# Four dense units a layer in the GLA fronts instead of the RWKV beats, and modulation products in four column groups

## The chip, the cores and the metric

The kernel runs on one core of a Trainium2 chip. Its time is device time in microseconds (us) from the start of the program to its end, the median of three runs. TensorE multiplies matrices, ScalarE (ACT) and VectorE (DVE) work on elements, GpSimd (POOL) does little here, and SyncE (SP) issues the DMA transfers of the weights. Every tensor is float32.

## The reference, cut to what matters

Two layers of a trunk with three parallel branches (RWKV-7, gated linear attention, latent attention) run over 128 context tokens and 512 latent tokens. The kernel handles both as 640 columns.

```python
def adaln_project(x, cvec, norm_g, w_mod, b_mod, w_in):
    mod = (jax.nn.silu(cvec) @ w_mod + b_mod)[:, None, :]      # the modulation: 1024 -> 3072
    shift, scale, gate = jnp.split(mod, 3, axis=-1)
    h = rmsnorm(x, norm_g) * (1 + scale) + shift
    return h @ w_in, gate                                      # the dense projections
# layer_forward: proj is split into r, k, v, g ... of RWKV, q, k, v, g of GLA, qd, kvd, g of MLA, merge
    o_a, st_rw = rwkv7_branch(...)     # a scan over tokens, done in chunks of 128
    o_b, st_gla = gla_branch(...)      # chunks with decay, two directions
    ...                                # MLA: attention over latents and a cache
    y = (g_a * y_a + g_b * y_b + g_c * y_c) @ lp['w_out']
    return x + gate * y, (ckv, ml_kpe, st_rw, st_gla)
```

## The kernel before, in words

Activations stand transposed, as 128 channels by 640 tokens. Weights come as **units** of 128 x 1024 numbers (512 KB) through `ring`, a buffer of five units: SyncE issues unit n when TensorE has released unit n - 5. The order of all units is fixed in `STREAM`, made by `unit_order`. A **dense unit** gives one tile of 128 output channels: eight products of 128 x 128 weights with 512 tokens, and eight with the other 128 tokens. In the profile each float32 product is two MATMUL records, and each transpose (L555) is one.

The stages of a layer, in order:

1. The modulation of layer 0 (`mod_product`, `mod_turn`, `mod_columns`), only at the start of the program. Six groups of 512 outputs; in each, eight products of a 128 x 2 weight block (`sc`, the two conditioning vectors) with 512 columns of a modulation unit add up in `psum[0:2]`. ScalarE copies the two rows to `con_sb`, TensorE turns them into columns by four transposes, and VectorE copies those to `mod_new`. The transfers of `hT` (the tokens) and `small_sb` are issued by GpSimd when groups 0 and 4 are filled.
2. RWKV. 20 steps (`STEPS`, four pairs of heads by five chunks) and one more for the tail; each step has 13 **beats** (`SLOTS`). In a beat TensorE does `rounds(q, j)`, the j-th link of a dependent chain of small products that go through ScalarE or VectorE after each link, and `chain(q - 1, j)`, then `beat()`: what `beat_work` has put there. That is a tile (one 512-token product of a dense unit of `DENSE`); behind a unit's eighth tile come its eight 128-token products, the **rest part**. In layer 0, products of layer 1's modulation stand there too.
3. The units `kvd` and `gg` 0, then the **GLA fronts**, one for each (p, d): TensorE computes `gx` (16 rows), projects the unit `GLA_KEYS[p, d]`, waits for `dve_ki`, transposes the keys (`kit`), waits for ScalarE's copy of them, computes the state products `gs` (128x64 tiles), and then for each of seven or eight levels j the small products `att` j, which need `dve_kq` j, followed by a tile of the unit `GLA_LEVEL[p, d]`. VectorE makes `ki`, `level(0)`, `level(1)`, the gate of the projected unit, the four states from `gs`, and then in a loop over j `kq` j and `level(j + 2)`. ScalarE's `Exp` of a level stands between `level(j)` and `kq` j.
4. MLA, the branch outputs with their merge gates, and `w_out`.

PSUM banks go round in `ticket`, which waits until the bank's last content has been taken out. A matmul whose output has at most 32 rows is placed on the column group of the array that its first PSUM row names, so `psum[0:2]` is always the first of four.

## Time and profile before

| what | value |
|---|---|
| median of 3 runs | 2998.87 us (2989.98 to 3000.86) |
| time of the profiled execution | 3000.72 us |
| its span, first to last instruction | 2998.9 us |
| TensorE busy | 2708.9 us, 90% |
| VectorE busy, ScalarE busy | 1153.9 us, 1000.0 us |
| RWKV beats, layer 0 and layer 1 | 110.8 to 806.6 us, 1603.0 to 2231.5 us |
| GLA fronts, layer 0 and layer 1 | 825.7 to 1004 us, 2251.9 to 2428 us |

The profiled execution took 1.85 us more than the median, and 1.8 us of its time lie outside its span. The stages are told apart by the forms of TensorE's instructions: small products of 32 x 32 are the beats, and 16-row products begin a front. A matmul's end in the profile is modelled and lies some 0.17 us behind the start of what follows it in a stream, so from start to start is the better measure of a short stretch.

### The profile page before, as it was taken

Reading aid. Unit: us, or ns where it says so; the run is one execution under the profiler, and the core shown is the slowest. Engines: PE = TensorE matmul, PEld = TensorE weight load, DVE = VectorE, ACT = ScalarE, POOL = GpSimd, SP = SyncE. Lnnn points to the kernel's source line nnn. Section 1 sums busy time; section 2 is a strip of 40 time slices with the busy share of each in tenths; the row PEclk is TensorE's granted clock in tenths of the full one; section 3 lists DMA queues with packets and bytes.
Section 4 is the critical chain, followed back from the end, with each engine's and each line's share of the span. In section 5 each row is a group of like instructions: output and inputs, shape, how many; then the busy total and the mean of one; then the engine's idle time right before and its main releaser. Section 6 shows DMA issues by size and latency. Waiting matters only on the chain.

```text
span 2998.9 us, 77811 instructions
## 1 busy us (share of the span) xinstructions
PE 2708.9 (90%) x35084; PEld 1643.0 (55%) x35084; DVE 1153.9 (38%) x2873; ACT 1000.0 (33%) x2108; POOL 28.6 (1%) x58
## 2 busy tenths in 40 slices
PE   8988989898987899999999898889998789999997
PEld 2555555555555555555555565556655555555554
DVE  1343444453265443311133445445436544331112
ACT  1333433443254434200014444435325444420000
POOL 0000000000000000000000000000000000000000
PEclk9998999999989899999999999999998889999999
DMA  8101010111110000222231000000010100012221
GB/s 299 44 30 46 31 44 32 45 33 44 52 30 30 20 22 15 86 70 70 78 97 37 24 26 24 18 24 26 17 39 30 30 20 22 15 45 70 71 76 63
DMA packets 35961, 141.95 MB, mean 47 GB/s; under 512 B 4592, under 2 KB 4624, under 8 KB 35248
## 3 DMA queue, kind: packets, MB, share of 16 engines
q1 hardware_dynamic: 31968, 115.82, 12.4%
q0 software_dynamic: 3664, 21.14, 2.0%
q8 instruction: 280, 4.59, 0.6%
q14 instruction: 49, 0.40, 0.0%
HBM read 129.97 MB, written 6.98 MB: 46 GB/s over the span
## 4 chain that ended last, share of the span: by engine, by line
PE 78%; ACT 9%; DVE 9%; issue 3%; DMA 1%; POOL 0%; ACTq 0%; DVEq 0%; SPq 0%
PE psum L552 74%; PE psum L555 4%; DVE tmp L1511 2%; DVE tmp L1503 1%; ACT tmp L1478 1%; DVE tmp L1500 1%; ACT tmp L1202 1%; ACT acts L1202 1%; ACT L1197 1%; DVE tmp L1600 1%; DVE tmp L1507 1%; DMA ring<-units 1%; ACT tmp L1342 0%; ACT L1193 0%; ACT tmp L1193 0%
## 5 line engine op out<-in xcount | busy, mean ns | idle before, releaser
L552 PE MATMUL psum<-hT,ring 128*128 128x128 f32 (+1 forms) x3904 | 1206.1, 453 | 16.7 <-DVE hT L1508 7.6
L552 PEld LDWEIGHTS psum<-hT,ring 128*128 128x128 f32 x3904 | 589.2, 195 | 377.8 <-issue 350.8
L552 PE MATMUL psum<-tmp 64*32 64x32 f32 (+7 forms) x11264 | 599.7, 245 | 66.0 <-DVE tmp L1503 24.3
L552 PEld LDWEIGHTS psum<-tmp 64*32 64x32 f32 (+4 forms) x11264 | 460.1, 134 | 196.7 <-issue 78.0
L1202 ACT ACTIVATE acts<-psum 128x128 f32<-128x128 f32 (+5 forms) x378 | 129.3, 354 | 580.1 <-PE psum L552 578.9
L552 PEld LDWEIGHTS psum<-acts 32*32 32x32 f32 x16320 | 180.5, 106 | 242.6 <-issue 90.5
L552 PE MATMUL psum<-acts 32*32 32x32 f32 x16320 | 222.8, 195 | 64.2 <-ACT acts L1202 24.2
L1202 ACT ACTIVATE tmp<-psum 128x512 f32<-128x512 f32 (+6 forms) x366 | 184.1, 505 | 275.5 <-PE psum L555 226.9
L552 PE MATMUL psum<-acts,ring 128*128 128x512 f32 (+1 forms) x768 | 210.8, 434 | 0.0
L555 PE MATMUL psum<-con_sb,tmp 128*128 128x128 f32 x760 | 130.5, 289 | 76.7 <-DVE tmp L1503 28.9
L1503 DVE TENSOR_TENSOR tmp<-tmp,psum 128x640 f32<-128x640 f32 x32 | 26.3, 821 | 375.4 <-ACT tmp L1490 205.9
L1490 ACT ACTIVATE tmp<-psum 128x640 f32<-128x640 f32 x32 | 22.5, 704 | 443.5 <-PE psum L552 443.5
L552 PEld LDWEIGHTS psum<-acts,ring 128*128 128x128 f32 x768 | 117.3, 191 | 92.1 <-issue 92.1
L555 PEld LDWEIGHTS psum<-con_sb,tmp 128*128 128x128 f32 x760 | 87.2, 144 | 128.3 <-issue 54.1
L552 PE MATMUL psum<-tmp,ring 128*128 128x512 f32 (+1 forms) x512 | 138.8, 434 | 0.0
L1500 DVE TENSOR_TENSOR tmp<-tmp 128x320 f32<-128x320 f32 (+3 forms) x264 | 125.6, 508 | 5.4
L1500 DVE TENSOR_TENSOR acts<-psum,acts 128x128 f32<-128x128 f32 (+1 forms) x160 | 51.7, 323 | 195.6 <-PE psum L552 194.3
L1503 DVE TENSOR_TENSOR tmp<-tmp 128x256 f32<-128x256 f32 (+2 forms) x216 | 89.7, 449 | 92.8 <-ACT tmp L1262 46.9
L1503 DVE TENSOR_TENSOR acts<-psum,con_sb 128x256 f32<-128x256 f32 x80 | 24.9, 352 | 238.1 <-PE psum L552 238.1
L552 PEld LDWEIGHTS psum<-tmp,ring 128*128 128x128 f32 x512 | 77.4, 191 | 61.2 <-issue 61.2
L552 PE MATMUL psum<-ring,sc 128*2 128x512 f32 x192 | 96.2, 620 | 9.3 <-DMA ring<-units 9.3
L1503 DVE TENSOR_TENSOR tmp<-tmp,acts 128x320 f32<-128x320 f32 (+2 forms) x208 | 96.1, 488 | 17.6 <-ACT g_dec L1404 12.2
(154 smaller groups left out, 1943.3 us busy)
## 6 DMA issues: line engine op xcount, KB each, us to landing
ring<-units SPq DMA_DIRECT2D x218, 512.0 KB, 3.6
small_sb<-small POOLq DMA_DIRECT2D x2, 3072.0 KB, 11.6
hT<-xT POOLq DMA_DIRECT2D x1, 2560.0 KB, 12.6
tmp<-xT POOLq DMA_DIRECT2D x8, 320.0 KB, 4.7
x_keep<-hT POOLq DMA_DIRECT2D x8, 320.0 KB, 4.9
tmp<-x_keep POOLq DMA_DIRECT2D x8, 320.0 KB, 3.4
yT<-acts POOLq DMA_DIRECT2D x8, 320.0 KB, 3.2
new_rw<-tmp POOLq DMA_DIRECT2D x8, 128.0 KB, 2.0
```

The source lines that it names most:

```text
L552: return nc.tensor.matmul(out, lhsT, rhs, start=start, stop=stop, skip_group_check=True)
L555: return nc.tensor.transpose(out, in_, ident[0:p, 0:p])
L1197: return nc.scalar.activation(out, out, ACT.Exp, scale=-0.5)
L1202: nc.scalar.activation(out, src, ACT.Copy).then_inc(act_e.sem, act_e.mark(key))
L1478: nc.scalar.activation(m_p[n % 3][:, 0:w], psum[:, at:at + w], ACT.Exp, bias=m_nm[:, n:n + 1], accum_out=m_sum[:, n:n + 1]).then_inc(act_e ...
L1490: nc.scalar.activation(f_s[j], psum[:, at:at + T], ACT.Sigmoid).then_inc(act_e.sem, act_e.mark((key, l, n)))
L1500: return V.tensor_tensor(out, a, b, op)
L1503: return V.tensor_tensor(out, a, b, ALU.mult)
L1507: return V.tensor_scalar(out, a, s1, None, op0)
L1511: return V.scalar_tensor_tensor(out=out, in0=a, scalar=s, in1=b, op0=op0, op1=op1)
L1600: ins = V.tensor_tensor_scan(w_z[:, z, :], gate[:, 0:P], w_z[:, z + 1, :], 0.0, ALU.mult, ALU.add if d == 0 else ALU.subtract)
```

## The change

Four units, `gv` 2, `gv` 3, `qd` 0 and `qd` 1, leave `DENSE`, which has 20 units instead of 24 over the same 273 beats. Each front now projects two units instead of one. `g` 2 moves one place ahead. VectorE's states move from ahead of the loop over the levels to behind `level(3)` in it. In the modulation, a step is now four products, one to each column group (`psum[32 * i:32 * i + 2]`), and two such steps make a group: each column group adds up two of the eight. ScalarE copies four pieces of two rows, into `acts`, and the turn is four products of those 128 rows with a constant that adds up the four pieces. The two units of a step are taken in one beat. VectorE clears the rows once at the start.

```diff
 FIRST_ITEMS = [("wdad", 0), ("k", 0), ("r", 0), ("v", 0)]
 DENSE = [("k", 1), ("r", 1), ("v", 1), ("g", 0), ("k", 2), ("r", 2), ("v", 2), ("misc", 0), ("g", 1), ("gq", 0),
-         ("k", 3), ("r", 3), ("v", 3), ("gq", 1), ("g", 2), ("gk", 0), ("gk", 1), ("gv", 0), ("g", 3), ("gv", 1),
-         ("gv", 2), ("gv", 3), ("qd", 0), ("qd", 1)]
+         ("k", 3), ("r", 3), ("v", 3), ("g", 2), ("gq", 1), ("gk", 0), ("gk", 1), ("gv", 0), ("g", 3), ("gv", 1)]
 END_ITEMS = [("kvd", 0)]
 REST_ITEMS = [("gg", 0)]
 
-GLA_KEYS = {(0, 0): ("gg", 1), (0, 1): ("mg", 0), (1, 0): ("mg", 1), (1, 1): ("mg", 2)}
+GLA_KEYS = {(0, 0): (("gg", 1), ("gv", 2)), (0, 1): (("mg", 0), ("gv", 3)), (1, 0): (("mg", 1), ("qd", 0)),
+            (1, 1): (("mg", 2), ("qd", 1))}
 GLA_LEVEL = {(0, 0): ("gg", 2), (0, 1): ("gg", 3), (1, 0): ("mg", 3), (1, 1): ("ma", 4)}
 MLA_MERGE = [("ma", n) for n in (0, 1, 2, 3, 5, 6, 7)]
...
@@ -94,8 +94,8 @@
     for q, (it, k) in enumerate(tiles):
         work[q * BEATS // len(tiles)].append((it, k))
     if l + 1 < DEPTH:
-        for i in range(MOD_GROUPS * KT):
-            work[(2 * i + 1) * BEATS // (2 * MOD_GROUPS * KT)].append((("mod", i // KT), i % KT))
+        for i in range(2 * MOD_GROUPS):
+            work[(2 * i + 1) * BEATS // (4 * MOD_GROUPS)].append((("mod", i // 2), i % 2))
     return work
...
@@ -105,12 +105,13 @@
     order = [(l, it) for it in FIRST_ITEMS]
     for beat in beat_work(l):
         for it, k in beat:
-            if it[0] == "mod" and k % 2 == 0:
-                order.append((l + 1, ("mod", 4 * it[1] + k // 2)))
+            if it[0] == "mod":
+                order += [(l + 1, ("mod", 4 * it[1] + 2 * k + i)) for i in range(2)]
             elif it[0] != "mod" and k == 0:
                 order.append((l, it))
     order += [(l, it) for it in END_ITEMS + REST_ITEMS]
-    order += [(l, it[pd]) for pd in GLA_KEYS for it in (GLA_KEYS, GLA_LEVEL) if pd in it]
+    for pd in GLA_KEYS:
+        order += [(l, it) for it in (*GLA_KEYS[pd], GLA_LEVEL[pd])]
...
@@ -482,8 +487,8 @@
                     sp.dma_start(vec[:, :], a["vec"][l]).then_inc(s_vec, 16)
                 if n >= RING:
                     ol, (old, oi) = STREAM[n - RING]
-                    if old == "mod" and oi % 4 < 3:
-                        sp.wait_ge(used.sem, used[(ol, oi)])
+                    if old == "mod" and oi % 4 < 2:
+                        sp.wait_ge(used.sem, used[(ol, oi // 4)])
                     elif old == "mod":
                         sp.wait_ge(filled.sem, filled[("modrow", ol, oi // 4)])
...
@@ -596,16 +601,17 @@
                 if k == 0:
                     grown["at"] = ticket(pe, ("modrow", l, j), 1, "act")
                     book["held"].add(grown["at"] // 512)
-                if k % 2 == 0:
-                    grown["w"] = unit(2)
-                    unit_done()
                 at = grown["at"]
-                last = mm(psum[0:2, at:at + 512], sc[:, k, :], grown["w"][:, k % 2, :], k == 0, k == KT - 1)
-                if k == KT - 1:
+                for i in range(4):
+                    if i % 2 == 0:
+                        w = unit(2)
+                        unit_done()
+                    last = mm(psum[32 * i:32 * i + 2, at:at + 512], sc[:, 4 * k + i, :], w[:, i % 2, :], k == 0, k == 1)
+                if k == 1:
                     last.then_inc(filled.sem, filled.mark(("modrow", l, j)))
                     book["held"].discard(at // 512)
-                elif k % 2 == 1:
-                    last.then_inc(used.sem, used.mark((l, 4 * j + k // 2)))
+                else:
+                    last.then_inc(used.sem, used.mark((l, j)))
...
@@ -645,7 +651,8 @@
                 pe.wait_ge(act_e.sem, act_e[("modrow", l, j)])
                 at = ticket(pe, ("mod", l, j), 1, "dve")
                 for i in range(4):
-                    last = tr(psum[:, at + 2 * i:at + 2 * i + 2], mod_row(j)[:, P * i:P * i + P], 2)
+                    last = mm(psum[:, at + 2 * i:at + 2 * i + 2], mod_row(j)[:, P * i:P * i + P],
+                              con[:, C_PICK:C_PICK + 2], True, True)
                 last.then_inc(filled.sem, filled.mark(("mod", l, j)))
...
@@ -932,7 +939,7 @@
                     for it, k in next(work):
                         if it[0] == "mod":
                             mod_product(l + 1, it[1], k)
-                            if k == 2 and it[1]:
+                            if k == 0 and it[1]:
...
@@ -976,7 +983,8 @@
                         at = ticket(pe, ("gx", l, p, d), 2, "dve")
                         w = small[0:16, SM["gla_a2"] + 256 * d + P * p:SM["gla_a2"] + 256 * d + P * p + P]
                         wide(at, w, item("misc")[0:16, :]).then_inc(filled.sem, filled.mark(("gx", l, p, d)))
-                        project(l, GLA_KEYS[p, d])
+                        for it in GLA_KEYS[p, d]:
+                            project(l, it)
...
@@ -1224,9 +1232,12 @@
                     act.wait_ge(filled.sem, filled[("mod", l, j - 2)])
                 act.wait_ge(filled.sem, filled[("modrow", l, j)])
                 at = place(("modrow", l, j))
-                copy(("modrow", l, j), mod_row(j), psum[0:2, at:at + 512])
+                for i in range(4):
+                    ins = nc.scalar.activation(mod_row(j)[32 * i:32 * i + 2, :], psum[32 * i:32 * i + 2, at:at + 512], ACT.Copy)
+                ins.then_inc(act_e.sem, act_e.mark(("modrow", l, j)))
 
...
 @@ -1859,21 +1874,22 @@
                         dve.wait_ge(dve_ki.sem, dve_ki[l, p, d])
                         level(0)
                         level(1)
-                        gates([GLA_KEYS[p, d]])
-
-                        dve.wait_ge(filled.sem, filled[("gs", l, p, d)])
...
+                        gates(GLA_KEYS[p, d])
+
+                        def states():
+                            dve.wait_ge(filled.sem, filled[("gs", l, p, d)])
...
@@ -1902,6 +1918,8 @@
                                 dve.wait_ge(dve_kq.sem, dve_kq[l, p, d, j])
                             if j + 2 < 7:
                                 level(j + 2)
+                            if j == 1:
+                                states()
                             if j > 2:
                                 attention(j - 1)
```

TensorE in layer 0's beats, before: the third of the beats that hold a modulation product (`psum<-ring,sc`). Counts here are products, not records; `psum<-hT,ring` is a dense unit's.

```order
L552 MATMUL psum<-tmp 128x128 x2
L552 MATMUL psum<-tmp 64x128 x4
L552 MATMUL psum<-tmp 128x128 x4
L552 MATMUL psum<-hT,ring 128x512
L552 MATMUL psum<-ring,sc 2x512
L552 MATMUL psum<-acts 32x32 x48
L552 MATMUL psum<-tmp 128x256 x4
L552 MATMUL psum<-hT,ring 128x512
L552 MATMUL psum<-acts 32x32 x32
L552 MATMUL psum<-acts,small_sb 128x128 x4
```

The same engine after the change, around the third step of modulation products, which stands in the step q = 4:

```order
L557 MATMUL psum<-tmp 128x256 x4
L557 MATMUL psum<-hT,ring 128x512
L557 MATMUL psum<-acts 32x32 x32
L557 MATMUL psum<-acts,small_sb 128x128 x4
L557 MATMUL psum<-acts 32x32 x16
L557 MATMUL psum<-tmp 64x128 x4
L557 MATMUL psum<-hT,ring 128x512
L557 MATMUL psum<-ring,sc 2x512 x4
L557 MATMUL psum<-con_sb,acts 128x2 x4
L557 MATMUL psum<-acts 32x32 x16
L557 MATMUL psum<-tmp 128x64 x4
L557 MATMUL psum<-acts 32x32 x32
```

Before, single modulation products stood behind the tile of 48 beats; now four stand together in 12 beats, and the turn (`con_sb,acts 128x2`) follows five of them. Before, the turn was four transposes (L555).

TensorE in the first GLA front of layer 0, from `gx` to the first tile of `GLA_LEVEL`, before:

```order
L552 MATMUL psum<-acts,small_sb 128x512
L552 MATMUL psum<-acts,small_sb 128x128
L552 MATMUL psum<-hT,ring 128x512 x8
L552 MATMUL psum<-hT,ring 128x128 x8
L555 MATMUL psum<-con_sb,tmp 128x128 x5
L552 MATMUL psum<-tmp 64x128 x10
L552 MATMUL psum<-tmp 64x64 x10
L552 MATMUL psum<-hT,ring 128x512
L552 MATMUL psum<-hT,ring 128x128
```

and after:

```order
L557 MATMUL psum<-acts,small_sb 128x512
L557 MATMUL psum<-acts,small_sb 128x128
L557 MATMUL psum<-hT,ring 128x512 x8
L557 MATMUL psum<-hT,ring 128x128 x8
L557 MATMUL psum<-hT,ring 128x512 x8
L557 MATMUL psum<-hT,ring 128x128 x8
L560 MATMUL psum<-con_sb,tmp 128x128 x5
L557 MATMUL psum<-tmp 64x128 x10
L557 MATMUL psum<-tmp 64x64 x10
L557 MATMUL psum<-hT,ring 128x512
L557 MATMUL psum<-hT,ring 128x128
```

A second unit of 8 + 8 products stands ahead of the transposes `kit`.

VectorE in the same front, from `level(0)` to the fourth level, before:

```order
L1500 TENSOR_TENSOR tmp<-tmp 128x5x64 x2
L1500 TENSOR_TENSOR tmp<-tmp 128x10x32 x2
L1503 TENSOR_TENSOR acts<-acts,psum 128x640
L1868 MEMSET tmp 128x128
L1869 COPY tmp<-small_sb 128x128
L1511 SCALAR_TENSOR_TENSOR tmp<-tmp,g_dec,psum 128x128 x3
L1875 COPY tmp<-psum 128x128
L1876 MEMSET tmp 128x1
L1503 TENSOR_TENSOR tmp<-tmp,acts 128x5x64 x2
L1500 TENSOR_TENSOR tmp<-tmp 128x20x16 x2
L1503 TENSOR_TENSOR tmp<-tmp,acts 128x10x32 x2
L1500 TENSOR_TENSOR tmp<-tmp 128x40x8 x2
```

and after:

```order
L1513 TENSOR_TENSOR tmp<-tmp 128x5x64 x2
L1513 TENSOR_TENSOR tmp<-tmp 128x10x32 x2
L1516 TENSOR_TENSOR acts<-acts,psum 128x640
L1516 TENSOR_TENSOR tmp<-tmp,acts 128x5x64 x2
L1513 TENSOR_TENSOR tmp<-tmp 128x20x16 x2
L1516 TENSOR_TENSOR tmp<-tmp,acts 128x10x32 x2
L1513 TENSOR_TENSOR tmp<-tmp 128x40x8 x2
L1884 MEMSET tmp 128x128
L1885 COPY tmp<-small_sb 128x128
L1524 SCALAR_TENSOR_TENSOR tmp<-tmp,g_dec,psum 128x128 x3
L1891 COPY tmp<-psum 128x128
L1892 MEMSET tmp 128x1
```

The states (from MEMSET 128x128 to MEMSET 128x1) stood ahead of `kq` 0 (`tmp<-tmp,acts 128x5x64`), and now stand behind `level(3)` (`tmp<-tmp 128x40x8`).

## Rows read from the trace of the kernel before

**Rows 1.** The page: its head and busy time by engine:
```profile
span 2998.9 us, 77811 instructions
PE 2708.9 (90%) x35084; PEld 1643.0 (55%) x35084; DVE 1153.9 (38%) x2873; ACT 1000.0 (33%) x2108; POOL 28.6 (1%) x58
```

**Rows 2.** Windows: length, busy by engine, then granted clock, DMA share, GB/s:
```profile
110.80:806.60 695.80, 626.76 (x12464) 388.20 (x12464) 293.40 (x898) 263.62 (x709) 2.18 (x4) 0.97 0.12 39
825.70:904.50 78.80, 64.48 (x1187) 40.78 (x1186) 51.87 (x110) 39.91 (x51) 0.00 (x0) 0.85 0.10 28
1603.00:2231.50 628.50, 569.78 (x12347) 380.47 (x12348) 291.28 (x892) 260.68 (x703) 2.17 (x4) 0.98 0.08 23
2251.90:2329.00 77.10, 62.96 (x1186) 39.69 (x1186) 51.35 (x109) 39.33 (x50) 0.00 (x0) 0.89 0.09 28
```

**Rows 3.** Groups by line of TensorE, 110 to 807 us (busy, mean ns, idle before):
```profile
L552 PE MATMUL psum<-hT,ring 128*128 128x512 f32 x384 | 217.5, 650 | 3.5 <-issue 2.0 <-DVE acts L1503 1.0 <-ACT acts L1202 0.3
...
L552 PE MATMUL psum<-ring,sc 128*2 128x512 f32 x96 | 49.6, 598 | 0.0
L552 PE MATMUL psum<-hT,ring 128*128 128x128 f32 x384 | 47.7, 278 | 1.5 <-ACT con_sb L1202 1.5
```

**Rows 4.** Timeline of TensorE in the RWKV beats of layer 1 (start, length, instruction):
```profile
1654.34 0.45 PE L552 MATMUL psum<-acts 64*64 64x64 f32 x8
1655.44 1.16 PE L552 MATMUL psum<-tmp 128*128 128x128 f32 x8 [0.65 <-ACT tmp L1202]
...
1700.18 1.30 PE L552 MATMUL psum<-tmp 128*128 128x128 f32 x12
1701.41 0.45 PE L552 MATMUL psum<-acts 32*32 32x32 f32 x32
...
1713.37 0.45 PE L552 MATMUL psum<-acts 64*64 64x64 f32 x8
1713.74 1.13 PE L552 MATMUL psum<-hT,ring 128*128 128x512 f32 x2
1714.71 1.05 PE L552 MATMUL psum<-tmp 128*128 128x128 f32 x8
```

**Rows 5.** Timeline of TensorE in one GLA front of layer 1:
```profile
2290.63 8.92 PE L552 MATMUL psum<-hT,ring 128*128 128x512 f32 x32
2303.11 0.76 PE L555 MATMUL psum<-con_sb,tmp 128*128 128x128 f32 x5 [3.57 <-DVE tmp L1503]
2304.67 2.40 PE L552 MATMUL psum<-tmp 128*64 128x128 f32 x20 [0.79 <-ACT tmp L1202]
2309.77 1.33 PE L552 MATMUL psum<-tmp 64*64 64x64 f32 x20 [2.69 <-DVE tmp L1503]
```

**Rows 6.** Waits of TensorE, fronts of layer 0 (total us, times, longest):
```profile
PE psum L555 <- DVE tmp L1503: 15.3, 4, 5.9
```

**Rows 7.** Timeline of ScalarE in the same front:
```profile
2304.64 1.28 ACT L1411 ACT_TABLE_LOAD   x1
2305.93 1.36 ACT L1411 ACTIVATE tmp<-tmp 128x640 f32<-128x640 f32 x2
```

**Rows 8.** Timeline of VectorE in the same front:
```profile
2307.46 1.11 DVE L1511 SCALAR_TENSOR_TENSOR tmp<-tmp,g_dec,psum 128x128 f32<-128x128 f32 x3
```

**Rows 9.** Timeline of TensorE, tiles of 64 columns in the attention:
```profile
1130.99 1.53 PE L552 MATMUL psum<-tmp 128*64 128x128 f32 x24 [0.68 <-ACT tmp L1202]
```

**Rows 10.** Timeline of TensorE, tiles of 32 by 32 in a beat:
```profile
1640.43 0.75 PE L552 MATMUL psum<-acts 32*32 32x32 f32 x64
```

**Rows 11.** Timeline at the end of the first stage:
```profile
58.77 7.03 PE L552 MATMUL psum<-ring,sc 128*2 128x512 f32 x16
...
65.89 0.59 ACT L1202 ACTIVATE con_sb<-psum 2x512 f32<-2x512 f32 x1 [4.17 <-PE psum L552]
...
66.97 0.17 DVE L1516 COPY mod_new<-psum 128x8 f32<-128x8 f32 x1 [0.64 <-PE psum L555]
```

**Rows 12.** A window in the first stage while the weights come in:
```profile
20.00:25.00 5.00, 4.08 (x13) 0.83 (x11) 0.00 (x0) 0.59 (x1) 0.00 (x0) 1.00 0.97 399
```

More of the change, by code:

```diff
@@ L178, in constant_table @@
         c[:, C_BIAS + j] = b
+    for r in range(0, P, 32):
+        c[r, C_PICK] = c[r + 1, C_PICK + 1] = 1.0
     i, j = np.arange(P)[:, None] % 32, np.arange(32)[None, :]
@@ L248, in mod_row @@
         def mod_row(j):
-            return con[0:2, C_COS + 512 * (j % 2):C_COS + 512 * (j % 2) + 512]
+            return small_of(MR + 512 * (j % 2), 512)
         def v(name, i=0, p=slice(0, P)):
@@ L660, in _ @@
             for j in range(MOD_GROUPS):
-                for k in range(KT):
+                for k in range(2):
                     mod_product(0, j, k)
@@ L1363, in beat @@
                     for it, k in next(work):
-                        if it[0] == "mod" and k == KT - 1:
-                            mod_out(l + 1, it[1])
-                        elif it[0] != "mod" and k == KT - 1:
+                        if it[0] == "mod":
+                            if k == 1:
+                                mod_out(l + 1, it[1])
+                        elif k == KT - 1:
                             project_parts(l, it)
@@ L1786, in beat @@
                     for it, k in next(work):
[L1787 to L1789 removed]
+                        if it[0] == "mod":
+                            if k == 0 and it[1]:
+                                mod_columns(l + 1, it[1] - 1)
+                        elif k == KT - 1:
                             gates_parts(it)
@@ L1861, in _ @@
                         level(1)
-                        gates([GLA_KEYS[p, d]])
-                        dve.wait_ge(filled.sem, filled[("gs", l, p, d)])
-                        at = place(("gs", l, p, d))
-                        o = SM["s_gla"] + P * (2 * d + p)
-                        order = (0, 1, 2, 3) if d == 0 else (3, 2, 1, 0)
-                        V.memset(g_st[d][:, 4, :], 0.0)
-                        V.tensor_copy(g_st[d][:, order[0], :], small[:, o:o + P]).then_inc(dve_step.sem, dve_step.mark())
@@ L1870, in _ @@
-                        dve.wait_ge(dve_step.sem, dve_step.n)
-                        for i, j in zip(order, order[1:]):
-                            stt3(g_st[d][:, j, :], g_st[d][:, i, :], g_dec[:, i:i + 1],
-                                       psum[:, at + P * i:at + P * i + P], ALU.mult, ALU.add).then_inc(dve_step.sem, dve_step.mark())
-                            dve.wait_ge(dve_step.sem, dve_step.n)
-                        V.tensor_copy(g_new[:, 2 * p + d, :], psum[:, at + 4 * P:at + 5 * P]).then_inc(dve_e.sem, dve_e.mark(("gs", l, p, d)))
@@ L1876, in _ @@
-                        V.memset(g_x[:, 0:1], 0.0).then_inc(dve_gstates.sem, dve_gstates.mark(l, p, d))
+                        gates(GLA_KEYS[p, d])
+                        def states():
+                            dve.wait_ge(filled.sem, filled[("gs", l, p, d)])
+                            at = place(("gs", l, p, d))
+                            o = SM["s_gla"] + P * (2 * d + p)
+                            order = (0, 1, 2, 3) if d == 0 else (3, 2, 1, 0)
+                            V.memset(g_st[d][:, 4, :], 0.0)
+                            V.tensor_copy(g_st[d][:, order[0], :], small[:, o:o + P]).then_inc(dve_step.sem, dve_step.mark())
+                            dve.wait_ge(dve_step.sem, dve_step.n)
+                            for i, j in zip(order, order[1:]):
+                                stt3(g_st[d][:, j, :], g_st[d][:, i, :], g_dec[:, i:i + 1],
+                                           psum[:, at + P * i:at + P * i + P], ALU.mult, ALU.add).then_inc(dve_step.sem, dve_step.mark())
+                                dve.wait_ge(dve_step.sem, dve_step.n)
+                            V.tensor_copy(g_new[:, 2 * p + d, :], psum[:, at + 4 * P:at + 5 * P]).then_inc(dve_e.sem, dve_e.mark(("gs", l, p, d)))
+                            V.memset(g_x[:, 0:1], 0.0).then_inc(dve_gstates.sem, dve_gstates.mark(l, p, d))
```

15 lines of the change are left out of this document (9 added, 6 removed).

## The prediction

> **What bounds the kernel now.** I read the page first: TensorE is busy for 2708.9 of 2998.9 us, VectorE and ScalarE for little more than a third [rows 1]. So TensorE's stream is the path nearly everywhere, and the change is judged by what leaves that stream and by which waits take its place. Then I read windows by stage. In the RWKV beats TensorE is busy for 626.8 of 695.8 us in layer 0 and 569.8 of 628.5 us in layer 1; in the first two GLA fronts of layer 0 for only 64.5 of 78.8 us, and there the granted clock is 0.85 against 0.97 and 0.98 in the beats [rows 2]. The groups by line say what fills the beats: dense tiles for 217.5 us and rest parts for 47.7 us in layer 0, and 48 modulation products (96 records) for 49.6 us [rows 3].
>
> The timeline shows what a filler is worth. Between two links of the chain a tile costs TensorE about 0.97 us (1713.74 to 1714.71). Without one there are two kinds of beats [rows 4]. In a quick one (beats 0 to 3, 5 and 12) the next group starts at once: 12 records at 1700.18 are followed at 1701.41. In a slow one (beats 4 and 6 to 11) TensorE waits for ScalarE or VectorE: beat 10 took 1.10 us empty (1654.34 to 1655.44) and 1.34 us filled (1713.37 to 1714.71), so the tile there costs 0.24 us.
>
> A front has the opposite shape. TensorE ends its unit about 8.65 us after 2290.63 and then waits 3.57 us for VectorE's `ki`; from the transposes at 2303.11 to level 0 at 2309.77 it waits another 0.79 and 2.69 us [rows 5]. The four waits for `ki` in layer 0 sum to 15.3 us [rows 6].
>
> **The change, part by part.** Sums are made against the profiled execution, 3000.7 us, which lies 1.9 us over the median.
>
> *Modulation products in the beats of layer 0.* 49.6 us go [rows 3]. What do four products in four column groups cost? A record of 512 columns takes 0.43 us (16 in 7.03 us) [rows 11], so each product is 0.86 us. If the four overlap fully, a step is 0.87 us plus two changes of tile shape of about 0.1 us: 1.05 us. If not at all, 3.6 us; if two at a time, 1.9 us. No row has four column groups under 128 rows. The nearest are these. With tiles of 64 columns, 24 records of 128 columns took 1.53 us, 0.064 us each [rows 9], against 1.30 us for 12 of full width, 0.108 us each [rows 4]: two run at once. With tiles of 32 x 32, 64 records took 0.75 us, 0.012 us each [rows 10], where 32 columns at 0.43/512 us each would need 0.027 us: at least 2.3 at once. I take the full overlap, since both kinds come close to the number of tiles that can be told apart: 12 steps x 1.05 = 12.6 us. The turn grows from four transposes to eight records; at 1.05 us for eight (1714.71) [rows 4] it costs some 0.5 us more, five times, 2.5 us. The row copies are four of 0.59 us instead of one [rows 11]; three of the six stand in beat 8, where TensorE soon waits for ScalarE, and 1.8 us more there, with 0.5 us hidden, costs 3.9 us. Sum: -49.6 + 12.6 + 2.5 + 3.9 = **-30.6 us**.
>
> The Trainium skill (TensorE: Matmul & The Clock Gate, Part 3) gives 2.38 times for three tiles of 32 columns. By that a step would be an estimated 1.4 to 1.5 us and this part some 5 us smaller; no row here shows three or four column groups.
>
> *The first stage.* Before, the last columns are out at 66.97 us, and TensorE was the limit: 7.03 us for each of six groups [rows 11]. With groups of about 2 us the transfers are the limit: 24 units (12.6 MB), `con` 0.95, `hT` 2.6, `masks` 0.5 and `small` 3.1 MB make 19.8 MB, at the 399 GB/s of a full window [rows 12] 49.5 us, from about 3.5 us on. The last step of products, four copies (2.4 us), the turn and VectorE's copy add 4.7 us: 57.7 us, **-9.3 us**. The clearing of the rows lies ahead of the first unit's landing and costs nothing; it could cost 1 us.
>
> *Dense units out of the beats.* Each layer loses 32 tiles and 4 rest parts. By the order of the beats, 11 of the 30 more empty beats in steps 0 to 19 are quick ones and 19 slow ones; the other two stand in the tail and are quick. Quick: 13 x 0.95 = 12.4 us, of which I take back 3 us, since an empty beat lets the next link ask VectorE sooner. Slow: 19 x 0.35 = 6.7 us (beat 10 gives 0.24, others up to 0.6). Rest parts: 47.7/24 less 0.2 us of modelled tail, 1.8 us each [rows 3], 7.2 us. Together 23.3 us a layer, **-46.6 us**.
>
> *Two units in a front.* A second unit is 8.65 us of TensorE by the first (2290.63 to its end, 8.92 us with its tail) [rows 5]: 34.6 us a layer. It hides under the 15.3 us that TensorE waits for `ki` [rows 6]; 19.3 us stay. `kit` then starts later than `ki` is ready, and VectorE has long made `level(0)` and `level(1)`. What is late next is ScalarE: its copy ends 1.5 us after `kit` starts, then a table load of 1.28 us and an `Exp` of 0.7 us [rows 7], and 0.9 us of `kq` 0. Level 0 can start 4.6 us after `kit`, where it was 6.66 us, because the states (1.11 us and four small instructions) [rows 8] no longer stand ahead: -2.06 x 4 = -8.2 us. The states now delay `kq` 2, but before, `Exp` and `kq` were late there too; I take -0.85 x 4 = -3.4 us. Sum: +7.7 us a layer, **+15.4 us**.
>
> Total: 3000.7 - 30.6 - 9.3 - 46.6 + 15.4 = 2929.6, so **2930 us**.
>
> **Bounds.** Modulation steps: up to 3.6 us each, +30.6 us, and then the first stage gains nothing, +9.3 us. As far down as the difference of the two layers' beats, 67.3 us [rows 2] against the 49.6 us of the records: -17.7 us. The units leaving the beats are worth between their rest parts with the quick tiles alone (+14 us) and their whole price, (217.5 + 47.7)/24 = 11.05 us each (-42 us). Fronts: from nothing (-15.4 us, if the waits ahead of level 0 are covered too) to +19.3 us a layer (+23.2 us, if moving the states gives nothing).
>
> **The rivals.**
> 1. *The column groups overlap in pairs or not at all.* For: nothing in the trace has four under 128 rows. Against: [rows 9, 10]. 2940 us in pairs, 2969 us one at a time. Chance 0.10.
> 2. *The second unit lies on the fronts' path.* VectorE and ScalarE do as much after `kit` as before, and each level's VectorE work (about 2 us) leaves it little slack. Then 2953 us, or 2964 us if the third level is late by the states besides. Against: the waits of 0.79 and 2.69 us [rows 5] are of just this kind and shrink. Chance 0.11.
> 3. *More comes back.* The beats of layer 0 fall by the 67.3 us that part them from layer 1's [rows 2], and continuous work ahead of `kit` keeps the clock up in the fronts. 2900 us. Chance 0.12.
> 4. *The clock falls in the thinned beats* (the other side). In the fronts, with waits of 3 us, it is 0.85 [rows 2]. Between layer 0's fronts at 0.85 (78.8 us) and layer 1's at 0.89 (77.1 us) lie 1.7 us, so a loss of x in the clock costs about 0.55 x of a stretch. In 1324 us of beats a fall to 0.87 costs 73 us and eats the whole gain; below 0.87 the kernel is slower. Against: a tile still stands in 160 of 273 beats, and TensorE's longest waits there come from the pair's norm and not from empty beats. Chance 0.14: 0.05 for slower by over 0.5%, 0.03 for no difference, 0.06 for a part of it, around 2955 us.
>
> The same page of the Trainium skill (TensorE: Matmul & The Clock Gate, HAM oscillation) says that idle stretches between bursts bring the half clock back, which speaks against thinning the beats. The fronts' 0.85 agrees with it.
>
> **How the numbers follow.** My own forecast has 0.53, between 2905 and 2955 us. The range 2895 to 2970 us takes in rivals 1 to 3 and the part of rival 4, and leaves some 0.15 outside, most of it above. A difference of 0.5% (15 us) is about what a measurement here can tell. Faster: 0.53 + 0.10 + 0.11 + 0.12 + 0.06 = 0.92; same 0.03; slower 0.05.
>
> **What would show it.** Right: records of `ring,sc` in the beats that start a few ns apart in fours, their busy time near 11 us instead of 49.6; last `mod_new` copy near 58 us; beats of layer 1 near 605 us and of layer 0 near 642 us; in a front `kit` about 17.4 us after the first unit starts, with no wait for `ki`, and level 0 about 4.6 us behind `kit`. Wrong: modulation records 0.43 us apart (rival 1), a front longer by more than 3 us (rival 2), a granted clock under 0.95 in the beats (rival 4), or waits in empty quick beats.

## The result, and the profile after

The changed kernel takes 2972.7 us (median of 6 runs, 2961.4 to 2983.4) against 2996.3 for the kernel before. The ratio is 0.992, 95% interval 0.990 to 0.994: a gain of 24 us where 71 was forecast, just outside the range. The profiled execution is the slowest of the six, 2983.4 us; the sums below are made against it, as the forecast was against 3000.7. Its granted clock was 0.959, where the middle ones of the six runs had 0.965 and 0.966.

The page of after, head and busy time:

```profile
span 2981.6 us, 77925 instructions
PE 2672.9 (90%) x35132; PEld 1653.3 (55%) x35132; DVE 1153.9 (39%) x2874; ACT 1023.1 (34%) x2138; POOL 28.6 (1%) x58
```

Windows of after, in the order of [rows 2] (length, busy by engine, granted clock, DMA share, GB/s):

```profile
104.60:772.40 667.80, 579.93 (x12360) 385.18 (x12360) 291.38 (x896) 273.55 (x721) 2.19 (x4) 0.93 0.11 36
791.50:876.50 85.00, 75.35 (x1251) 46.55 (x1250) 51.58 (x110) 40.93 (x53) 0.00 (x0) 0.98 0.13 39
1579.30:2203.70 624.40, 546.34 (x12211) 369.39 (x12212) 290.31 (x890) 258.48 (x696) 2.17 (x4) 0.95 0.07 20
2224.10:2308.90 84.80, 75.14 (x1250) 45.99 (x1250) 51.09 (x109) 40.24 (x52) 0.00 (x0) 0.98 0.13 38
```

The clock has changed sides. In the beats it was 0.97 and 0.98 [rows 2] and is 0.93 and 0.95; in the fronts it was 0.85 and 0.89 and is 0.98. Layer 0's beats are 28 us shorter where 54 was forecast, layer 1's 4 us where 23 was.

Groups by line in layer 0's beats, after, against [rows 3]:

```profile
L557 PE MATMUL psum<-hT,ring 128*128 128x512 f32 x320 | 196.7, 701 | 0.3 <-DVE acts L1516 0.2
...
L557 PE MATMUL psum<-hT,ring 128*128 128x128 f32 x320 | 40.2, 280 | 0.0
...
L557 PE MATMUL psum<-ring,sc 128*2 128x512 f32 x96 | 13.2, 622 | 0.7 <-ACT acts L1210 0.7
```

The tiles are a sixth fewer, but one record of 512 columns is busy for 701 ns instead of 650, at a granted clock of 0.93 instead of 0.97. The 96 modulation records are busy for 13.2 us instead of 49.6. One whole step of eight records in the timeline of TensorE:

```profile
131.50 1.04 PE L557 MATMUL psum<-ring,sc 128*2 128x512 f32 x8 [0.69 <-ACT acts L1210]
132.47 0.33 PE L560 MATMUL psum<-con_sb,tmp 128*128 128x128 f32 x1
```

A step takes 0.97 us from start to start; in the trace its records start in fours, 6 to 7 ns apart, and the second four 0.42 us behind the first. What one tile (two records) costs, in layer 1's beats at the full clock (2.4 GHz) and at the half clock (1.2 GHz):

```profile
1865.37 1.12 PE L557 MATMUL psum<-hT,ring 128*128 128x512 f32 x2
1866.42 0.75 PE L557 MATMUL psum<-acts 32*32 32x32 f32 x64
...
1877.97 2.08 PE L557 MATMUL psum<-hT,ring 128*128 128x512 f32 x2
1879.97 0.28 PE L557 MATMUL psum<-acts 32*32 32x32 f32 x3
```

1.05 us from start to start at 2.4 GHz, 2.00 us at 1.2 GHz. A second front of layer 1 after, against [rows 5]:

```profile
2268.52 17.57 PE L557 MATMUL psum<-hT,ring 128*128 128x512 f32 x64
2285.93 0.71 PE L560 MATMUL psum<-con_sb,tmp 128*128 128x128 f32 x5
2287.48 1.31 PE L557 MATMUL psum<-tmp 128*64 128x128 f32 x20 [0.84 <-ACT tmp L1210]
2290.46 0.80 PE L557 MATMUL psum<-tmp 64*64 64x64 f32 x20 [1.66 <-DVE tmp L1516]
...
2295.63 0.89 PE L557 MATMUL psum<-tmp 64*32 64x32 f32 x80 [1.34 <-DVE tmp L1516]
```

kit starts 17.4 us after the first unit with no wait for ki, and level 0 4.5 us behind it, both as forecast. The last line is `att` 2, the third level: it now waits 1.34 us for VectorE, which makes the states just before that level's `kq`; in the same front before, it did not wait.

**Where the 17.3 us between the two profiled executions are.** Boundaries are the first instruction of a stage on TensorE. First stage 110.8 to 104.6: -6.2. Layer 0's beats with the units behind them: -28.0. Its fronts +11.5. Layer 1's beats -4.1, fronts +10.1. All else -0.6.

### The profile page after: what moved, and what is told of

The parts are those of the page before. It is cut to its first block, busy times and chain, and to the rows that moved or that the text cites. A ratio compares the mean times of both kernels' runs of the same rounds, so it can differ in the third digit from the quotient of the medians.

```text
span 2981.6 us, 77925 instructions
## 1 busy us (share of the span) xinstructions
PE 2672.9 (90%) x35132; PEld 1653.3 (55%) x35132; DVE 1153.9 (39%) x2874; ACT 1023.1 (34%) x2138; POOL 28.6 (1%) x58
## 4 chain that ended last, share of the span: by engine, by line
PE 79%; ACT 9%; DVE 7%; issue 3%; DMA 1%; POOL 0%; SPq 0%; ACTq 0%; DVEq 0%
PE psum L557 75%; PE psum L560 4%; DVE tmp L1516 2%; ACT tmp L1491 1%; DVE tmp L1524 1%; DVE tmp L1513 1%; ACT acts L1210 1%; ACT tmp L1210 1%; DMA ring<-units 1%; ACT L1205 1%; DVE tmp L1614 1%; ACT tmp L1353 1%; DVE acts L1513 0%; ACT tmp L1201 0%; ACT L1201 0%
## 5 line engine op out<-in xcount | busy, mean ns | idle before, releaser
L557 PE MATMUL psum<-acts 32*32 32x32 f32 x16320 | 230.0, 197 | 91.0 <-DVE acts L1513 31.3
L1665 DVE COPY_PREDICATED tmp<-masks_sb,psum 128x512 f32<-128x512 uint8 x120 | 82.4, 721 | 30.9 <-PE psum L557 30.9
```

What stands on the lines that cost most here:

```text
L557: return nc.tensor.matmul(out, lhsT, rhs, start=start, stop=stop, skip_group_check=True)
L1665: return V.copy_predicated(gbuf(q, name).rearrange("p (d h) x -> p d h x", d=2), masks[:, m, :, :].unsqueeze(2).broadcast_to([P, 2, 2, P]) ...
```

## The experiments

Two theories for the beats. **C, the clock**: a removed tile is worth what the forecast says, but the thinned stream of TensorE is granted the half clock more often. **W, waits**: the removed tiles only filled time in which the chain waited anyway. The table gives, for the beats of steps 0 to 18 (247 of the 273), the length and the time at the half clock in the profiled execution of each kernel, added up from the clock's intervals in the trace (a window shows the same as its granted clock: 1579.3 to 2163.5 us at 0.95 is 584 x 2 x 0.05).

| kernel | median us, ratio to before | layer 0: us, of it at half clock | layer 1 |
|---|---|---|---|
| before | 2993 to 2998 | 647.4, 44.4 | 585.9, 23.9 |
| after | 2972.7, 0.992 | 622.6, 95.6 | 584.2, 61.4 |
| mod_alone | 2960.7, 0.988 (0.986 to 0.990) | 619.7, 30.7 | 582.9, 20.5 |
| dense_alone | 2982.5, 0.995 (0.993 to 0.997) | 617.8, 41.0 | 581.1, 64.9 |
| dummy_slow | 2972.9, 0.991 (0.989 to 0.994) | 608.9, 27.3 | 582.8, 20.5 |
| thin | 2982.9, 0.996 (0.994 to 0.997) | 627.3, 170.7 | 591.7, 150.2 |
| tiles_slow | 2895.4, 0.967 (0.965 to 0.968) | 575.3, 34.1 | 544.3, 20.5 |
| mod_slow | 2918.8, 0.975 (0.973 to 0.976) | 608.8, 44.4 | 574.5, 37.5 |

Some profiled executions are not typical of their kernel: after's (2983.4 us) is the slowest of six, dense_alone's (2974.4) the fastest of eight, and mod_slow's (2945.1) lies 26 us over its median.

The windows behind it: before, after, mod_alone, dense_alone, dummy_slow, thin and tiles_slow, two layers each.

```profile
110.80:758.20 647.40, 579.04 (x11765) 360.21 (x11766) 278.30 (x860) 250.95 (x678) 1.64 (x3) 0.97 0.12 38
1603.00:2188.90 585.90, 527.63 (x11663) 352.71 (x11665) 277.32 (x855) 248.48 (x673) 1.62 (x3) 0.98 0.08 23
```
```profile
104.60:727.20 622.60, 538.52 (x11682) 359.18 (x11682) 276.83 (x858) 258.39 (x687) 1.64 (x3) 0.92 0.11 36
1579.30:2163.50 584.20, 509.24 (x11554) 345.20 (x11554) 276.46 (x853) 246.35 (x667) 1.63 (x3) 0.95 0.07 20
```
```profile
102.50:722.10 619.60, 546.12 (x11786) 357.82 (x11786) 278.21 (x860) 260.10 (x693) 1.64 (x3) 0.98 0.12 39
1563.10:2146.00 582.90, 525.21 (x11663) 352.23 (x11665) 277.50 (x855) 248.18 (x673) 1.62 (x3) 0.98 0.08 23
```
```profile
110.30:728.10 617.80, 544.38 (x11665) 346.33 (x11668) 277.21 (x858) 249.08 (x672) 1.64 (x3) 0.97 0.12 37
1576.40:2157.50 581.10, 509.37 (x11552) 344.57 (x11553) 276.21 (x853) 246.09 (x667) 1.62 (x3) 0.94 0.07 21
```
```profile
106.30:715.20 608.90, 554.39 (x11770) 357.24 (x11770) 276.82 (x858) 258.94 (x687) 1.65 (x3) 0.98 0.11 37
1564.20:2147.00 582.80, 537.42 (x11653) 350.36 (x11654) 276.34 (x853) 247.01 (x667) 1.63 (x3) 0.98 0.07 20
```
```profile
102.00:729.30 627.30, 513.73 (x11572) 358.93 (x11572) 276.67 (x858) 257.95 (x687) 1.64 (x3) 0.86 0.11 36
1576.00:2167.70 591.70, 485.26 (x11448) 346.08 (x11449) 275.87 (x853) 246.18 (x667) 1.62 (x3) 0.87 0.07 20
```
```profile
103.00:678.30 575.30, 515.90 (x11685) 348.75 (x11686) 275.74 (x858) 257.29 (x687) 1.64 (x3) 0.97 0.12 38
1526.60:2070.90 544.30, 495.33 (x11556) 339.45 (x11556) 275.30 (x853) 245.19 (x667) 1.62 (x3) 0.98 0.07 22
```

**Each part alone.** Of the changed kernel, mod_alone takes back `DENSE`, `GLA_KEYS` and the place of the states; dense_alone has these and the modulation of before.

```diff
 mod_alone, against after
+         ("gv", 2), ("gv", 3), ("qd", 0), ("qd", 1)]
+GLA_KEYS = {(0, 0): (("gg", 1),), (0, 1): (("mg", 0),), (1, 0): (("mg", 1),), (1, 1): (("mg", 2),)}
-                            if j == 1:
-                                states()
```

> Only the modulation part of the change: products four at a time in column groups; the dense units stay in the beats as before, and the states ahead of the loop. It computes everything. In the changed kernel the first stage gave 6.2 us and both layers' beats much less than forecast. If the thinned beats lose to the clock (theory C) or if freed time was only cover for waits (theory W), the dense units are the poor part in both, and this part alone keeps nearly its forecast: layer 0's beats 647.4 - 31 = 616 us from the first beat of q = 0 to that of q = 19, layer 1's unchanged at 586 us, in all 2958 us. If it is the modulation part that fell short, 2975 us or more.

> Only the dense part: four units a layer in the fronts, states behind the fourth level; modulation products single, in 48 beats, as before. It computes everything. My forecast by itself would be 46.6 - 15.4 = 31 us less than before, 2965 us. Theory C (the clock falls in the thinned beats) and theory W (the freed time turns into waits for ScalarE and VectorE) both say that layer 1's beats stay near 584 us and the fronts cost 10 to 12 us a layer: 3005 to 3015 us, slower than before. C: half-clock time in layer 1's beats near 60 us instead of 24. In layer 0 the modulation products still fill 48 beats, so C says less loss there than in layer 1; W says the same.

Alone, the parts gain 37.5 and 15.7 us (2998.2 is the median of before beside them), 53 together; both at once gained about 25. The 28 us between them are certain to some 11 us, by the intervals of the three ratios. mod_alone came as expected. My expectation for dense_alone was wrong: it isn't slower than before. Layer 1's beats are as in after (581.1 and 64.9 at the half clock), but layer 0's are 29.6 us shorter than before, with no more half clock than before. There the single modulation products still stand in 43 of these beats. So the loss appears in layer 0 only when both fillers thin out, and with it 51 us more at the half clock than before (20 to 51 us in the executions of the next table). C says so; W has no place for it, since the tiles removed are the same. But W is not empty: in layer 1's beats TensorE's waits sum to 59 us before and 76 us after.

**More products, no more time.**

```diff
 dummy_slow, against after
+                    if not todo and grown["open"] and j in (4, 6, 7, 8, 9, 10, 11):
+                        at = grown["item_at"]
+                        mm(psum[:, at:at + TS], small_of(MR + 1024, P), hT[:, 0, 0:TS], False, False)
```

> The changed kernel with one added product (zero weights, 512 columns, added to the open sum, so every result stays) in each empty slow beat (4 and 6 to 11) while a unit's sum is open, some 17 a layer. By the price of a tile in a slow beat (0.24 to 0.6 us) it adds 6 us a layer of TensorE's path. Theory W: so it is slower by 10 us, about 2983. Theory C: the clock comes back in part, half-clock time in layer 1's beats falls from 61 us towards 35, at some 0.45 us for each us of half clock -12 us, and the layer is 6 us shorter: about 2961 us.

I had miscounted: it adds 50 products in layer 0 and 53 in layer 1, not 17; 45 and 48 of them stand in steps 0 to 18. With those 45 more, 39 us of TensorE's time, layer 0's beats are 13.7 us shorter than in after's profiled execution, and the half clock falls from 95.6 to 27.3 us. In layer 1 it falls from 61.4 to 20.5 and the beats are 1.4 us shorter. If an added tile costs d and a microsecond at the half clock costs c, then 45 d - 68.3 c = -13.7 and 48 d - 40.9 c = -1.4: c = 0.41, d = 0.32 us. (With 50 and 53 it came to 0.42, which the sums below keep.) The forecast had 0.35 for a tile in a slow beat. The whole is no slower with 103 useless products: 2972.9 us.

That c is about right can be seen without the added products. Four kernels have the same instructions of TensorE in these beats, and their executions differ in the clock:

| kernel | layer 0: us, of it at half clock | layer 1 |
|---|---|---|
| after | 622.6, 95.6 | 584.2, 61.4 |
| states_ahead | 618.0, 85.3 | 591.0, 78.5 |
| square_early | 617.7, 85.3 | 586.9, 64.9 |
| halves | 609.4, 64.9 | 588.1, 71.7 |

A line through the four gives 0.43 us for each us at the half clock in layer 0 and 0.36 in layer 1. Over all 124 runs whose granted clock is on record, each against the mean of its own kernel, it is 0.37 us, with a standard error of 0.02. The table also shows that after's own execution is the slowest in layer 0: dummy_slow's 608.9 us are only 0.5 us under the fastest, so what is shown is that the added products cost nothing, not that they save 14 us.

**Fewer products, more time.** thin leaves out products 1, 3 and 5 of each dense unit in the beats.

```diff
+                    if k not in (1, 3, 5):
+                        mm(psum[:, at:at + TS], w[:, k, :], hT[:, k, 0:TS], k == 0, k == KT - 1)
```

> The changed kernel with three of the eight 512-token products of each dense unit in the beats left out (60 a layer; the sums are then incomplete, the 128-token products stay). By the price of a tile without any effect of the clock, 0.6 us on average, it is shorter by 36 us a layer, 2900 us. Theory C: half-clock time in layer 1's beats goes from 61 us to over 100, which at 0.42 gives back 17 us or more of the 36: 2935 us, with the mean clock below the 0.96 of the changed kernel. Theory W: 2970 us, with waits longer by the 51 us that the products took.

120 tiles less, 103 us of products, and the kernel is 10 us slower than after. The clock over the whole run is 0.934, and layer 1's beats have 89 us more at the half clock: 0.42 x 89 = 37 us lost, against 7.5 us measured, so the 54 tiles missing there are worth 30 us, 0.55 each. Both theories said less time (2935 us by C, 2970 by W); C had the direction of the clock and not its size.

**The same tiles in other beats.**

```diff
 tiles_slow, against after
-        work[q * BEATS // len(tiles)].append((it, k))
+        slow = [b for b in range(BEATS) if 4 <= b % SLOTS < 12]
+        work[slow[q * len(slow) // len(tiles)]].append((it, k))
```

> The changed kernel with the same 160 tiles in other beats: only in beats 4 to 11 of each step (168 of them), so that nearly every beat in which the chain waits has a tile and beats 0 to 3 and 12 have none. It computes everything. By the price of a tile (0.95 us in a quick beat, 0.35 in a slow one), some 54 tiles a layer move from quick to slow beats: up to 0.6 x 54 = 32 us a layer less. Theory C (what the thinned beats lose, they lose to the clock, at 0.42 us for each us at half clock, as the two layers of the kernel with the added products give it): waits are covered, so half-clock time in layer 1's beats falls from 61 us towards 20, and both effects add up: 2900 us. Theory W (an empty quick beat gains nothing, since the chain is then late in the next slow link): the beats stay at 584 and 622 us, and the time near 2970 us.

> The kernel with the modulation part alone (all 24 dense units in the beats), with the tiles only in beats 4 to 12 (189 of them, 3 with two tiles). It computes everything. Some 45 tiles a layer move from quick to slow beats at 0.6 us each, the clock stays as high as it is there (20 to 31 us at half clock a layer): 2960 - 2 x 27 = 2906 us. If an empty quick beat gains nothing: 2960 us.

tiles_slow: 2895.4 us, where C said 2900 and W 2970. Layer 1's beats are 39.9 us shorter: 17 by the clock (40.9 us at 0.42) and 23 by the place of 49 tiles, 0.46 each where I took 0.6. mod_slow (with `b % SLOTS > 3`) gained 42 us on mod_alone where 54 was expected. The clock doesn't explain the 12 us: its 44 and 38 us at the half clock come from an execution 26 us over the median, and the middle ones of its runs had a granted clock of 0.967 and 0.968, mod_alone's 0.966. Why it gained less stays open. Between tiles_slow and mod_slow the dense part now brings 23 us; with the tiles spread evenly (after against mod_alone) it cost 12, with intervals that just meet. So the same edit has the other sign, by where the remaining tiles stand.

**The fronts.**

```diff
 states_ahead, against after
                         def states():
...
+                        states()
-                            if j == 1:
-                                states()
```

> The changed kernel with VectorE's states put back ahead of the loop over the levels. It computes everything. My sum took the move behind the fourth level for -2.06 us ahead of level 0 and -0.85 us later, in each of eight fronts: without it +23 us, 2996 us, with level 0 at 6.7 us behind kit instead of 4.5. Rival: the states only change their place in the chain of VectorE, and what level 0 gains is lost at the third level; then the end of a front stays where it is, and the time is 2973 to 2978 us.

2981.5 us, 9 us slower than after instead of 23. TensorE in the same front as above, from kit on:

```profile
2285.01 0.71 PE L560 MATMUL psum<-con_sb,tmp 128*128 128x128 f32 x5
2286.56 1.31 PE L557 MATMUL psum<-tmp 128*64 128x128 f32 x20 [0.84 <-ACT tmp L1210]
2290.56 0.80 PE L557 MATMUL psum<-tmp 64*64 64x64 f32 x20 [2.69 <-DVE tmp L1516]
...
2295.84 0.89 PE L557 MATMUL psum<-tmp 64*32 64x32 f32 x80
```

Level 0 stands 5.5 us behind kit, so the move itself gave 1.0 us there; the rest of the 6.66 us of before was the front's own lower clock: its state products took 2.40 us [rows 5] and take 1.31. The third level (last line) has no wait here, where after has 1.34 us: moving the states shifts a wait from level 0 to the third level. A front of after is 1.0 us shorter on average, but states_ahead's runs were also granted less clock (0.960 in the middle, after's 0.966), some 33 us more at the half clock, which alone is worth 12 us or more. So these runs don't show that the move gives anything at the same clock.

```diff
 halves, against after
-                        for it in GLA_KEYS[p, d]:
-                            project(l, it)
+                        project(l, GLA_KEYS[p, d][0])
+                        project_some(l, GLA_KEYS[p, d][1], range(4))
...
                         last.then_inc(filled.sem, filled.mark(("kit", l, p, d)))
+                        project_some(l, GLA_KEYS[p, d][1], range(4, 8))
```

> The changed kernel with the second unit of each front cut in two: four tiles ahead of the transposes kit, four behind them and ahead of the state products. It computes everything. VectorE's ki was ready before kit in the changed kernel (no wait there), and behind kit TensorE waits 0.8 us for ScalarE's copy and 1.9 us for level 0. Now kit stands 4.3 us earlier, the copy, the table load and Exp run under the other four tiles: level 0 follows the state products without a wait, 2.3 us less a front, -18 us in all, 2955 us. Rival: the fronts are bound by VectorE's work for the levels behind that, so the gain ends at the third level: 2970 us.

2943.8 us, 29 less than after, more than the 18 expected. The second front of layer 1:

```profile
2232.14 13.24 PE L557 MATMUL psum<-hT,ring 128*128 128x512 f32 x48
2245.22 0.71 PE L560 MATMUL psum<-con_sb,tmp 128*128 128x128 f32 x5
2245.77 4.49 PE L557 MATMUL psum<-hT,ring 128*128 128x512 f32 x16
2250.19 2.04 PE L557 MATMUL psum<-tmp 128*64 128x128 f32 x40
2252.16 1.35 PE L557 MATMUL psum<-hT,ring 128*128 128x512 f32 x4
```

State products and level 0 (x40) run in one piece with no wait, and the later levels' waits shrink too: a front ends 4.2 us sooner on average.

**Row copies and the first stage.**

```diff
 one_copy, against after, for layer 1's rows only
-                for i in range(4):
-                    ins = nc.scalar.activation(mod_row(j)[32 * i:32 * i + 2, :], psum[32 * i:32 * i + 2, at:at + 512], ACT.Copy)
+                    ins = nc.scalar.activation(mod_row(j)[0:98, :], psum[0:98, at:at + 512], ACT.Copy)
 square_early, against after
-                if j == MOD_GROUPS - 2:
+                if j == MOD_GROUPS - 3:
                     mean_square(0)
```

> The changed kernel with one ScalarE copy of 98 rows for layer 1's modulation rows in the beats instead of four copies of two rows (the rows between are multiplied by zero in the turn, so the results stay). My sum took 3.9 us for the longer copies, of which this gives back nearly all, 2969 us; the modulation part alone showed some 6 us more in layer 0's beats than the products and turns account for, then 2967 us. Rival: the copies are hidden, no change.

> The changed kernel with the mean square of the tokens (8.9 us of TensorE) behind the fourth group of modulation products instead of behind the fifth. It computes everything. In the changed kernel the last group's products stand 8.9 us behind it and the last columns are out at 61.3 us, where I had forecast 57.7 from the transfers alone. If that order is what the first stage missed, the squares now run while the units of the fifth group come in, the last columns are out near 57 us, and the whole is 4 us shorter: 2969 us. Rival: the ring of five units is held up by the squares, the transfers stop meanwhile, and the last columns stay at 61 us.

one_copy took 2970.8 us (ratio 0.992, 0.989 to 0.995): no difference can be told in the whole. In its trace layer 0's beats take 603.9 us with 64.9 us at the half clock, 5.5 us less than in halves with the same 64.9. square_early took 2976.0 us (0.993). Its last group of products:

```profile
51.09 1.03 PE L557 MATMUL psum<-ring,sc 128*2 128x512 f32 x4 [0.24 <-DMA ring<-units]
59.91 1.87 PE L557 MATMUL psum<-ring,sc 128*2 128x512 f32 x4 [7.80 <-DMA ring<-units]
```

The last unit came 7.8 us late, behind the transfer of `small`, which the fifth group's end releases.

**All together.** best has the tiles in beats 4 to 11, the halves and the early square; best_copy also the one copy; no_square is best_copy with the square in its old place; small_late is best_copy with `small` released by the sixth group.

> Tiles only in beats 4 to 11, the second unit of a front in halves around kit, and the squares early, all three on the changed kernel. It computes everything. If they add up: 2895 - 29 - 4 = 2862 us. If the halves owe part of their 29 us to chance in the clock of the beats (their fronts are 3.4 to 4.5 us shorter, eight times, at most 32), 2870 us.

> The same with the one copy of 98 rows in the beats of layer 0. With the tiles in beats 4 to 11 ScalarE's copies in beat 8 stand where the chain waits for it, so up to 4 us less than the kernel without it: 2858 us; if hidden, the same time.

> Tiles in beats 4 to 11, halves and one copy, with the mean square where the changed kernel has it, behind the fifth group. It computes everything. With the square early, the last unit of the first stage came 7.8 us later, behind the transfer of small, which the fourth group's end then releases sooner: the first beat began at 109.5 us against 104.6. So without it the whole is 3 to 5 us shorter than 2862: 2858 us. If the first stage's order is worth nothing: 2862 us.

> The same with the square early and the transfer of small released by the sixth group instead of the fifth, so that the last units of the modulation don't share the queues with it. It computes everything. If the two transfers' order was what held up the first stage, the last columns are out near 55 us instead of 61 and the first beat begins near 99 us: 2853 us. Rival: small is then late, and the first use of small in the RWKV preparation waits, so that nothing is gained.

| kernel | median us | ratio to before |
|---|---|---|
| best | 2879.4 | 0.961 (0.959 to 0.963) |
| best_copy | 2862.5 | 0.956 (0.954 to 0.958) |
| no_square | 2862.2 | 0.956 (0.954 to 0.958) |
| small_late | 2857.1 | 0.954 (0.952 to 0.956) |

The parts add up within 17 us for best, which starts its beats 4.5 us later than tiles_slow, for the reason just shown. Here one copy instead of four gave 17 us, 13 of it in layer 0's beats (579.8 to 566.8 us), with 20 us less at the half clock, some 9 us of the 13. In small_late the unit that was 7.8 us late comes in time:

```profile
52.64 1.03 PE L558 MATMUL psum<-ring,sc 128*2 128x512 f32 x4 [0.46 <-DMA ring<-units]
53.60 1.05 PE L558 MATMUL psum<-con_sb,acts 128*128 128x2 f32 x8
56.22 1.87 PE L558 MATMUL psum<-con_sb,acts 128*128 128x2 f32 x8 [1.56 <-ACT acts L1240]
```

So the order of the two transfers held up square_early, but the last columns are out at 58.1 us against 58.9 in no_square, not at 55: the order of the square is worth nothing that these runs can tell. The best kernel stands at 2857 us, 4.6% under before.

## Why the prediction was wrong, step by step

**The step that failed is "Dense units out of the beats", -46.6 us**, with rival 4's "Against: a tile still stands in 160 of 273 beats". The prices of the tiles were close; the sum put at nothing what thinning does to the clock of all that stays. Steps 0 to 18 of layer 1: measured -1.7 us, with 37.5 us more at the half clock, 16 us at 0.42; without it the removed tiles and rest parts gave some -17.5 us, where the same part of the forecast gives 20. Layer 0: measured -24.8 with 51.2 us more at the half clock, 21.5 us; without it -46, where both parts' forecasts give some -47. Together the clock took some 37 us of the 45 that the beats fell short in these two executions. This isn't the luck of one execution: on average over the four of the table above, layer 0 is 30.5 us shorter and layer 1 is 1.6 us longer than before, with 84 us more at the half clock, some 35 us, where these steps fall short of the forecast by 38. This is rival 4, in the branch that I gave 0.06 ("a part of it"), though 18 us above its 2955. The sign that I named for it, a clock under 0.95, came in layer 0's window; in layer 1 it stood at 0.95.

**Its price was too low as well.** I had 0.55 x of a stretch for a loss of x in the clock, from two fronts of each layer, in which TensorE is idle for 18% of the time (64.48 of 78.80 us busy) and whose clocks are only 0.04 apart. The beats gave 0.36 to 0.43 us per us at the half clock; 0.42 is 0.84 x.

**Modulation products, -30.6 us**: right. 49.6 went to 13.2 us busy, a step of 0.97 us where I took 1.05. The turns came to 3.2 us more, 2.5 forecast (TensorE start to start in steps 0 to 18: 1.7 and 4.9 us). mod_alone's layer 0 is 27.7 us shorter, 5.8 of it by a higher clock, so 21.9 against some 26 forecast for those steps. What the row copies cost in the changed kernel (3.9 in the sum) one_copy's median couldn't tell from nothing; its trace says 5.5. The Trainium skill (TensorE: Matmul & The Clock Gate, Part 3) has 2.38 times for three tiles of 32 columns; here the measurement differs: four took the time of one.

**First stage, -9.3 us**: -6.2 in this execution. The last columns are out at 61.3 us, not 57.7. TensorE shows where it went:

```profile
45.27 8.90 PE L557 MATMUL psum<-acts,con_sb 128*128 128x512 f32 x32
54.09 2.26 PE L557 MATMUL psum<-ring,sc 128*2 128x512 f32 x16
...
59.37 1.87 PE L557 MATMUL psum<-con_sb,acts 128*128 128x2 f32 x8 [2.04 <-ACT acts L1236]
```

The whole last group stands behind the mean square and starts 1.1 us after my end of the transfers, takes 2.2 us instead of one step, and the last turn runs at the half clock (1.87 us instead of 1.05). In no_square, with the same first stage, they are out at 58.9 us: over the ten kernels with this stage, the beats begin between 102.0 and 106.4 us, in seven of them by 103.0, so most executions gain nearly 8 us or more.

**Fronts, +15.4 us**: +21.6. The 17.4 us to kit and the 4.6 us behind it were right; the states' -0.85 us a front at later levels was not there, and the third level got a wait of 1.34 us instead. A front ended 18.8 (layer 0) and 18.5 us (layer 1) behind the start of level 0 before, and 19.4 and 18.0 us after. The higher clock in the fronts, half of rival 3, came true (95.6 us at the half clock before, 23.9 after, both layers) but is already inside these numbers: with it the move still cost more than I said. Over the whole kernel the clock of the middle runs was about 0.966 before and after: what the fronts got back, the beats lost.

Sum: 2929.6 + 45.1 (beats) + 3.1 (first stage) + 6.2 (fronts) - 0.6 (all else) = 2983.4, the profiled execution.

Open: what exactly in the stream makes the clock fall in one beat and not in another was not tried. c lies between 0.36 and 0.43 by the ways above, and dense_alone's layer 1, with the same beats, lies 5 us under the line of the four executions, so a stretch is understood to some 5 us and no better. One kernel's runs scatter by 8 to 30 us, so terms of a few us (copies, square) are read from the traces alone or not at all.

## What to carry to other kernels

A filler product between the links of a dependent chain has two prices: its own time where nothing waits, and the clock of everything around it. Before thinning a stream, read the granted clock of a stretch that is already thin, and put the fillers that remain under the waits first: that alone was worth 77 us here. Test two edits apart and together, since both thinning the same stream cost some 28 us that neither cost alone.

## What the runs showed of the hardware

- Four products of 128 x 2 weights and 512 columns, one to each column group, started 6 to 7 ns apart and took together what one takes, 0.42 us a record.
- The same tile took 1.05 us at 2.4 GHz and 2.00 us at 1.2 GHz, start to start, in one step of one execution.
- 103 us of products taken away made the kernel 10 us slower (thin), and 103 useless ones, some 89 us, made it no slower (dummy_slow, 2972.9 against 2972.7 us). The Trainium skill (TensorE: Matmul & The Clock Gate, HAM oscillation) describes idle stretches between bursts that bring the half clock back; the trace agrees in direction, 170.7 us at the half clock in layer 0's beats of thin against 27.3 in dummy_slow. The page's kernel waits for DMA, this one for ScalarE and VectorE, in after's layer 1 beats never longer than 3.3 us.
- A microsecond at the half clock cost 0.36 to 0.43 us in beats in which TensorE is busy for 86 to 87% of the time.
- A ScalarE copy of 98 rows of 512 took 0.60 us, as long as one of 2 rows (0.59 us).
